# Second block: token halves in turn, and its first feed-forward layer once over both at 512 columns

## The reference

```python
h = x * (1.0 + sc1) + sh1;  hc = xc * (1.0 + csc1) + csh1
y, yc = mixer(h, hc, ...)
x = _layer_norm(ALPHA * x + g1 * y, ln1_g, ln1_b)
h = x * (1.0 + sc2) + sh2
x = _layer_norm(ALPHA * x + g2 * _conv_ffn(h, w_up, conv_w, conv_b, w_down), ln2_g, ln2_b)
if need_ctx:            # first layer only: the same weights over the context's tokens
    xc = _layer_norm(ALPHA * xc + cg1 * yc, ln1_g, ln1_b)
    hc = xc * (1.0 + csc2) + csh2
    xc = _layer_norm(ALPHA * xc + cg2 * _conv_ffn(hc, ...), ln2_g, ln2_b)
```

## Time and profile before

| | |
|---|---|
| median of 3 runs | 2494.47 us (2494.15 to 2495.27) |
| profiled execution: time | 2492.11 us |
| its span | 2490.8 us, 41466 instructions |
| PE busy | 2289.4 us (92%), 18046 instructions |
| DVE / ACT busy | 1322.1 us (53%) / 1129.4 us (45%) |
| weight loads | 355 of 1 MB |
| HBM read | 376.87 MB |

### The profile page before, as it was taken

The page is one execution under the profiler, slowest core; times in us unless marked ns, Lnnn a source line. Parts: engine busy times, 40 slices in busy tenths (PEclk is TensorE's granted clock), DMA queues, the critical chain, the costliest instruction groups (busy, mean ns, idle before and its releaser), DMA issues.

```text
span 2490.8 us, 41466 instructions
## 1 busy us (share of the span) xinstructions
PE 2289.4 (92%) x18046; PEld 2074.7 (83%) x18046; DVE 1322.1 (53%) x1986; ACT 1129.4 (45%) x1754; POOL 54.4 (2%) x100
## 2 busy tenths in 40 slices
PE   6999989998999999899987998689989979997997
PEld 5998779997998899789975766489989956576997
DVE  3446565456555665365554256366666642355665
ACT  3444454436444643364445255254445531344544
POOL 0000000000000100000000000000000000000000
PEclk9999989999999899899998999899999989998999
DMA  8454535545544644255452110145444513203551
GB/s 311 175 190 178 209 138 197 198 158 220 187 170 177 231 172 164 92 204 188 171 203 83 68 51 35 51 152 194 174 166 178 187 67 124 96 18 113 192 191 46
DMA packets 55381, 381.00 MB, mean 153 GB/s; under 512 B 8480, under 2 KB 8864, under 8 KB 9248
## 3 DMA queue, kind: packets, MB, share of 16 engines
q1 hardware_dynamic: 51264, 373.32, 40.2%
q10 hardware_dynamic: 864, 4.63, 0.5%
q0 software_dynamic: 3072, 0.40, 0.1%
HBM read 376.87 MB, written 1.05 MB: 152 GB/s over the span
## 4 chain that ended last, share of the span: by engine, by line
PE 86%; DVE 8%; ACT 4%; DMA 1%; issue 1%; SPq 0%; POOL 0%; DVEq 0%; ACTq 0%
PE ps L551 18%; PE ps L552 17%; PE ps L553 17%; PE ps L682 5%; PE ps L332 3%; PE ps L333 2%; PE ps L334 2%; PE ps L1971 2%; PE ps L1972 2%; PE ps L1973 2%; PE ps L1213 1%; PE ps L748 1%; PE ps L735 1%; DVE wl L306 1%; PE ps L376 1%; PE ps L2241 1%
## 5 line engine op out<-in xcount | busy, mean ns | idle before, releaser
L306 DVE TENSOR_TENSOR wl<-ring,wh 128x1024 fp32r<-128x1024 f32 x538 | 631.2, 1221 | 303.3 <-ACT wh L302 302.8
L551 PE MATMUL ps<-xs,wh 128*128 128x256 f32 x2464 | 704.9, 286 | 57.4 <-DVE wl L306 51.3
L552 PE MATMUL ps<-xs,wl 128*128 128x256 f32 x2464 | 703.3, 285 | 0.0
L553 PE MATMUL ps<-xs,wh 128*128 128x256 f32 x2464 | 703.1, 285 | 0.0
L302 ACT ACTIVATE wh<-ring 128x1024 fp32r<-128x1024 f32 x538 | 534.9, 1049 | 177.4 <-PE ps L553 128.0
L551 PEld LDWEIGHTS ps<-xs,wh 128*128 128x128 f32 x2464 | 479.6, 195 | 61.8 <-DVE wl L306 47.6
L552 PEld LDWEIGHTS ps<-xs,wl 128*128 128x128 f32 x2464 | 479.5, 195 | 0.0
L553 PEld LDWEIGHTS ps<-xs,wh 128*128 128x128 f32 x2464 | 479.3, 195 | 0.0
L551 PE MATMUL ps<-hh,wh 128*128 128x256 f32 x1232 | 348.9, 283 | 2.2 <-DVE hl L649 2.2
L552 PE MATMUL ps<-hh,wl 128*128 128x256 f32 x1232 | 348.6, 283 | 0.0
L553 PE MATMUL ps<-hl,wh 128*128 128x256 f32 x1232 | 348.6, 283 | 0.0
(11 more groups left out here) (381 smaller groups left out, 2927.3 us busy)
## 6 DMA issues: line engine op xcount, KB each, us to landing
ring<-wstream SPq DMA_DIRECT2D x355, 1024.0 KB, 4.9
ada_rows<-ada_stage POOLq DMA_DIRECT2D x96, 4.0 KB, 4.4
CN<-consts ACTq DMA_DIRECT2D x1, 1136.0 KB, 15.5
X<-xin ACTq DMA_DIRECT2D x1, 1024.0 KB, 10.5
X<-cin ACTq DMA_DIRECT2D x1, 1024.0 KB, 9.1
out<-X SPq DMA_DIRECT2D x1, 1024.0 KB, 3.9
PT__59<-pin ACTq DMA_DIRECT2D x1, 512.0 KB, 18.9
ab_w<-wab ACTq DMA_DIRECT2D x1, 512.0 KB, 3.8
```

What stands on the lines that cost most here:

```text
L306: dve.tensor_tensor(wl[:, BUF[i], :, :], tile_of(i), wh[:, BUF[i], :, :].bitcast(F32), ALU.subtract).then_inc(low_part, 1)
L551: pe.matmul(out, wh[:, w, c, :], x_hi, start=start, stop=False, skip_group_check=True)
L552: pe.matmul(out, wl[:, w, c, :], x_hi, start=False, stop=False, skip_group_check=True)
L553: return pe.matmul(out, wh[:, w, c, :], x_lo, start=False, stop=True, skip_group_check=True)
```

## The change

In the second block:

- The output projection of the even mixer runs x's eight tiles and then the context's eight, each 256 columns wide; its third and fourth weight slots get high buffers of their own (`e_wh2`). x's mixer output is split during the last steps of the context's attention. The norm of x (`l0_1x`) is done while TensorE works on the context's tiles, the context's (`l0_1c`) while it works on x's first two gate/up tiles.
- Gain, bias and modulation are folded into one scale and one offset for each feature (`dve_ln_columns`), applied to `Z` directly. ALPHA times the norm's result is made in place in `Z` (`act_residual`).
- The first layer's FFN runs once: gate, up and the first four output blocks of down 512 columns wide over both halves (tiles 0 and 1 of gate/up half by half). PSUM has room for four of the eight output blocks only, so all hidden rows are kept, and the last four blocks are made after the loop, 11 double steps for x, then 11 for the context, 256 columns wide. During the context's steps x's second norm (`l0_2x`) is done; the context's (`l0_2c`) during the odd mixer's first tiles.
- This FFN has four weight buffers, and 40 loads in place of 66.
- `l1_1` takes the form of the first block's norms; in `l1_2` the last eight passes are shared by ScalarE and VectorE.

The core of the diff (new functions, then what calls them):

```diff
-        BUF.append((i - first) % 4 if first <= i < last else i % NB)
+        BUF.append((i - first) % 4 if first <= i < last else (i - both) % 4 if both <= i < both + 7 * NPAIR else i % NB)
         PREV.append(max((j for j in range(i) if BUF[j] == BUF[i]), default=None))
...
+        def dve_modulated_low(name, q):
+            k = x_parts(X_AFTER[name]) // 4 - XSPLITS.index("l0_x")
+            for c in (2 * q, 2 * q + 1):
+                g, b = ln_cols(name, c)
+                dve.wait_ge(z_normed, 4 * LNS.index(name) + q + 1)
+                dve.tensor_scalar(x_whole(name, c), Z[:, ln_half(name), c, :], g, b, ALU.mult,
+                                  ALU.add).then_inc(low_whole, 1)
+            dve.wait_ge(x_high, x_parts(X_AFTER[name]) + q + 1)
+            dve.wait_ge(low_whole, 8 * k + 2 * q + 2)
+            c = slice(2 * q, 2 * q + 2)
+            dve.tensor_tensor(x_target(name, 1, c), x_whole(name, c), x_target(name, 0, c).bitcast(F32),
+                              ALU.subtract).then_inc(x_low, 1)
...
+        def act_residual(name, c0=0, c1=KC):
+            n, j = LN_COLS.index(name[0:4]), ln_half(name)
+            if name in X_AFTER:
+                act.wait_ge(*x_split(X_AFTER[name]))
+                act.wait_ge(x_high, x_parts(X_AFTER[name]) + 4)
+            else:
+                act.wait_ge(h_made, KC)
+            for c in range(c0, c1):
+                z = act.activation(Z[:, j, c, :], Z[:, j, c, :], ACT.Identity, scale=ln_res[:, n, 0, c:c + 1],
+                                   bias=ln_res[:, n, 1, c:c + 1])
+            if c1 == KC:
+                z.then_inc(z_scaled, 1)
...
+            for t in range(16):
+                j = t // 8
                 if t >= 4:
-                    pe.wait_ge(z_done, Z0["l0_1"] + 2 * (t - 3))
-                return t % 4
-            for t in range(8):
-                pe_slot_tile(9 + t // 2, t % 2, bank_out(t), lambda c: e_yh[:, c, :], lambda c: e_yl[:, c, :],
-                             e_y_low if t == 0 else None)
+                    pe.wait_ge(z_done, Z0["l0_1x"] + t - 3)
...
+            def gate_or_up(t, k, j=None):
+                b, i = 4 + 2 * (t % 2) + k, gate_up_tile(t, k)
+                out, x = (ps[:, b, :], slice(0, 2)) if j is None else (ps[:, b, j * T:(j + 1) * T], j)
+                pe.wait_ge(low_part, i + 1)
+                for c in range(KC):
+                    mm = three(out, i, c, xc[:, x, c, 0, :], xc[:, x, c, 1, :], start=(c == 0))
+                return mm
+            def down(t):
+                i = F0 + 5 * (t // 2) + 4
+                pe.wait_ge(low_part, i + 1)
+                pe.wait_ge(hidden_low, G0 + t + 1)
+                for o in range(4):
+                    mm = three(ps[:, o, :], i, 4 * (t % 2) + o, fh[:, t % 2, :, :], fl[:, t % 2, :, :], start=(t == 0))
+                if t % 2:
+                    mm.then_inc(proj_done, 1)
+                elif t == NT - 2:
+                    mm.then_inc(f_down20, 1)
+            def last_down(j, k):
+                i = B0 + NPAIR * j + k
+                pe.wait_ge(low_part, i + 1)
+                pe.wait_ge(f_low, NPAIR * j + k + 1)
+                for o in range(4):
+                    for u in range(2):
+                        mm = three(ps[:, 4 + 2 * j + o // 2, (o % 2) * T:(o % 2 + 1) * T], i, 4 * u + o,
+                                   fh[:, (NPAIR * j + k) % 2, u, :], fl[:, (NPAIR * j + k) % 2, u, :],
+                                   start=(k == 0 and u == 0 and o % 2 == 0))
+                    if k == NPAIR - 1 and o == 1:
+                        mm.then_inc(f_bank, 1)
+                mm.then_inc(proj_done, 1)
+            pe.wait_ge(*x_split("l0_x"))
+            gate_or_up(0, 0, 0)
+            pe_mean("l0_1c")
+            gate_or_up(0, 1, 0)
+            gate_or_up(1, 0, 0)
+            pe_variance("l0_1c")
+            gate_or_up(1, 1, 0)
+            for c in range(KC):
+                if c % 2 == 0:
+                    pe.wait_ge(x_low, x_parts("l0_c") + c // 2 + 1)
+                for k in range(2):
+                    mm = three(ps[:, 4 + k, T:2 * T], gate_up_tile(0, k), c, xc[:, 1, c, 0, :], xc[:, 1, c, 1, :],
+                               start=(c == 0))
+            mm.then_inc(gate_up_done, 1)
+            gate_or_up(1, 0, 1)
+            gate_or_up(1, 1, 1).then_inc(gate_up_done, 1)
+            down(0)
+            for t in range(2, NT):
+                gate_or_up(t, 0)
+                gate_or_up(t, 1).then_inc(gate_up_done, 1)
+                down(t - 1)
+            down(NT - 1)
+            for k in range(NPAIR):
+                last_down(0, k)
+            for k in range(NPAIR):
+                last_down(1, k)
+                if k == 0:
+                    pe_mean("l0_2x")
+                if k == 4:
+                    pe_variance("l0_2x")
...
+            def hidden(t, ahead=()):
+                k, n = t % 2, G0 + t
+                act.wait_ge(gate_up_done, n + 1)
+                act.activation(fcg[:, k, :, :], ps[:, 4 + 2 * k, :].rearrange("p (j n) -> p j n", j=2), ACT.Identity,
+                               scale=pcol("l0_cw", NT + t), bias=pcol("l0_cb", t)).then_inc(conv_mid, 1)
+                for i in ahead:
+                    act_high(i)
+                act.wait_ge(conv_side, 2 * t + 2)
+                act.activation(fsg[:, k, :, :], fcg[:, k, :, :], ACT.Silu).then_inc(silu_done, 1)
+                buf, at = hidden_of(t)
+                act.wait_ge(hidden_done, n + 1)
+                act.activation(fh[:, k, :, :], buf[:, at, :, :], ACT.Copy).then_inc(hidden_high, 1)
+            def last_high(m):
+                j, k = divmod(m, NPAIR)
+                if m == 0:
+                    act.wait_ge(f_down20, 1)
+                else:
+                    name, value = TAKEN[F0 + 5 * NPAIR - 1 if m == 1 else B0 + m - 2]
+                    act.wait_ge(signal[name], value)
+                buf, at = hidden_of(2 * k)
+                act.activation(fh[:, m % 2, :, :], buf[:, at:at + 2, j, :], ACT.Copy).then_inc(f_high, 1)
+            hidden(0, [F0 + 4])
+            act_high(F0 + 5)
+            hidden(1)
+            act_residual("l0_1c")
+            act_high(F0 + 6)
+            act_high(F0 + 7)
+            for t in range(2, NT):
+                hidden(t)
+                i = F0 + 5 * (t // 2)
+                if t % 2 == 0:
+                    act_high(i + 3)
+                    act_high(i + 4)
+                    act_high(i + 5)
+                elif t < NT - 1:
+                    act_high(i + 6)
+                    act_high(i + 7)
+            act.preload_act_table_set("natural_log_exp_and_others")
+            last_high(0)
+            act_high(B0 + 1)
+            act_high(B0 + 2)
+            for m in range(1, 2 * NPAIR):
+                last_high(m)
+                if m + 2 < 2 * NPAIR:
+                    act_high(B0 + m + 2)
+                k = m - NPAIR
+                if k in (1, 2):
+                    act_square("l0_2x", 2 * k - 2)
+                    act_square("l0_2x", 2 * k - 1)
+                if k == 5:
+                    act_factor("l0_2x")
+                if 6 <= k < 10:
+                    act_modulated("l0_2x", 2 * (k - 6))
+                    act_modulated("l0_2x", 2 * (k - 6) + 1)
+            act_residual("l0_2x")
...
+            dve.wait_ge(ln_cols_made, 1)
             for t in range(8):
-                dve_add_branch("l0_out", "l0_1", t, 2, lambda j: MOD[:, 0, 16 + t, j:j + 1])
+                branch(0, t)
+            dve_low(F0)
+            for q in range(4):
+                dve_centre("l0_1x", q)
+            branch(1, 0)
+            for q in range(4):
+                dve_square_pair("l0_1x", q)
+            branch(1, 1)
+            dve_low(F0 + 1)
+            branch(1, 2)
+            dve_scaled("l0_1x", 0)
+            dve_scaled("l0_1x", 1)
+            dve_modulated_low("l0_1x", 0)
+            branch(1, 3)
+            dve_scaled("l0_1x", 2)
+            dve_modulated_low("l0_1x", 1)
+            branch(1, 4)
+            dve_scaled("l0_1x", 3)
+            dve_modulated_low("l0_1x", 2)
+            branch(1, 5)
+            dve_modulated_low("l0_1x", 3)
+            branch(1, 6)
+            branch(1, 7)
+            dve_layer_norm("l0_1c", None, (F0 + 2, F0 + 3))
...
+            z = Z0["l0_2"]
+            last_low(0)
+            dve_low(B0 + 1)
+            dve_low(B0 + 2)
+            dve.wait_ge(z_scaled, ZIN["l0_c"])
+            dve.wait_ge(*tile_done(B0 - 1))
+            for m in range(1, 2 * NPAIR):
+                last_low(m)
+                if m + 2 < 2 * NPAIR:
+                    dve_low(B0 + m + 2)
+                if m <= 4:
+                    for o in (0, 1) if m % 2 else (2, 3):
+                        dve_last_branch((m - 1) // 2, o)
+                if m in (5, 6):
+                    dve_pair("l0_2x", m - 5, z + 2 * (m - 4))
+                k = m - NPAIR
+                if k == 0:
```

(71 more changed lines are left out.)

563 lines of the change are left out of this document (377 added, 186 removed).

## The result

The changed kernel takes 2415.39 us (median of 4 runs, 2413.82 to 2416.07), the kernel before in the same measurement 2494.31 (2494.13 to 2495.27): ratio 0.9683, 95% interval 0.9671 to 0.9695. Forecast were 2418.7 in a range from 2408 to 2440. The gain is 78.9 us, 75.8 were worked out.

A forecast was written before the change was run, and what follows sets the result against it. TensorE was taken to bound the kernel, time being won at its waits or in shorter work. Gains of 68.5 (stretch), 6.8 (norm before the last FFN) and 0.5 (last norm) sum to 75.8, giving 2418.7 us, range 2408 to 2440.

The forecast's parts named there:

- The bound and the pitches: TensorE is 86% of the chain; 512 columns save 12.8 ns a pair, 15.7 us in all; the rest is seams.
- Attention tail: End of context attention: four copies and four subtractions moved into its last steps cost 2.0 us, bounds 0 to 2.8.
- Output projection: Even mixer: 16 tiles take 46.0 us plus 3.75 for statistics; x's norm hidden, ring slot eating 2 of 3 us spare.
- First two tiles: First FFN's gate/up by halves: 23.0 us, 3.75 for the context's statistics, and a 2.8 us wait for its parts.
- Main loop: First-layer FFN: gate/up 217.6 us, down 59.8; weight chain hidden with 1.3 us of slack, no wait, 13.6 us a tile.
- Rival 5: Main loop waits for weights in each tile, each microsecond past 8.2 costing 20; chance 0.04 mild, 0.02 in full.
- Residual: Loop tile one: eight `act_residual` passes ahead of a weight copy in ScalarE's queue make TensorE wait 3.2 us.
- low clock: Two falls of TensorE's clock after waits of 2.5 to 3 us cost 3.0 us, bounds 0 and 9.
- Last down tiles: After the loop: x's and context's last down tiles, waits and extra chain costing 8.0 us, bounds 3 and 20.
- Rivals 2 and 4: Clock falls for good in last context tiles, 2436, chance 0.08; all last down tiles take 4.8 us, 2453, chance 0.05.
- The stretch as a whole: End of even attention to the odd projection's sixth tile: 535.6 us before, 467.1 after, gain 68.5 us.
- Rival 1: Norms aren't hidden at the output projection: two exposed by 9 us each, 2437 us; chance 0.14.

The follow-up runs named there:

- e1: Changed kernel with each 512-column gate/up tile of the loop made as two 256-column halves: 2424.33 us, ratio 0.9720 to the kernel before.
- e5: Changed kernel with the variance of x's first norm made after the output projection's 15th tile instead of the 11th: 2419.76 us, ratio 0.9706 to the kernel before.
- e2b: Changed kernel with three idle ScalarE passes before the next weight copy in loop tiles 2 to 20: 2480.08 us, ratio 0.9944 to the kernel before.
- e3: Changed kernel with the residual's passes done two at a time behind later weight copies, in both FFNs: 2405.20 us, ratio 0.9644 to the kernel before.
- e4: Changed kernel with VectorE's centring and scaling ahead of the weight tile's low part in the context's last down tiles: 2404.59 us, ratio 0.9643 to the kernel before.
- e2a: Changed kernel with one idle ScalarE pass before the next weight copy in loop tiles 2 to 20: 2409.29 us.
- e7: Changed kernel with both the spread residual passes and VectorE's centring and scaling moved ahead in the context's last down tiles: 2399.40 us, ratio 0.9622 to the kernel before.

## Why the prediction was right, point by point

**The bound and the pitches.** Right in the pitches: e1 gives 13.1 ns a pair against 12.8. The 2.5 ns of the Trainium skill ("TensorE: Matmul & The Clock Gate", Back-to-back issue gap), which the page gives for the isolated gap of a matmul and not for a stream with its weight loads, is a fifth of what a pair of these matmuls saves by this trace and by e1. "The rest is seams" was wrong. The norms' statistics got cheaper too, since neighbouring blocks are now added before the matmuls: a mean of l0_2 before, and its context half after the change:

```profile
2018.31 7.03 PE L437 MATMUL ps<-Z,CN 128*128 128x512 f32 x16
```

```profile
1978.43 1.89 PE L509 MATMUL ps<-ln_sum,CN 128*128 128x256 f32 x8
```

Four such rows before and eight after make some 13 us less. The output projection lost 192 pairs, 2.5 us. So of the 78.4 us some 26 are less work for TensorE (16.0 + 13 - 2.5), 46.0 are waits, and most of the rest is low clock (an estimate from the clock over stretches of 1 us: 16 us lost before, 11 after). The forecast gain held in spite of it, because its sum counts the matmuls after the change and takes them from the whole stretch before.

**Attention tail, 2.0.** Mis-sized: 0.49. Most of the passes found idle time, so the truth lay near the lower of the bounds, 0 and 2.8.

**Output projection, 46.0 and 3.75.** Right: 49.60 us from 1537.48 to 1587.08, no wait. The x half was ready 48.6 us into the stretch, 1.0 before it was wanted, which is the forecast's 3 less the 2 that the ring slot eats. What was expected of e5 took the 3 as if nothing ate of it.

**First two tiles.** The wait before the context half is 1.6 in three pieces, not 2.8: the parts come 2.05, 2.04 and 1.44 us apart after the first, not 2.2. The first FFN matmul was forecast for 1588.6 and came at 1587.08.

**Main loop.** Right in its place and in its size: no wait, 13.6 us a tile, slack 1.1 to 1.4 where 1.3 had been worked out. What the forecast had wrong about the loop is the price beyond the edge: "each microsecond costs 20" is 37 by e2b (67.5 us for 1.81), since most waits have a fall of the clock behind them. Rival 5 was as unlikely as I said, but nearly twice as dear.

**Residual, 3.2; end of the loop, 2.5; low clock, 3.0.** 2.61, 2.58 and about 1.6 (one fall, 0.58 for 4.07 us; after the second wait of the same length the clock stayed at 1.00). e3 shows that the residual's eight passes are the cause of the first.

**Last down tiles, 8.0.** Measured 5.8 in five waits (0.51, 1.48, 1.07 and 1.35 in four of them), the later tiles 4.45 apart against 4.8 forecast. The mechanism was right, and e4 takes it away by order alone. Rivals 2 and 4 have fallen: the clock was 1.00 all through, and only five tiles waited. The Trainium skill's case of short idle spells (same page, A second HAM failure mode: psum-queue depth-cycling) doesn't strike at this spacing; in e2b's loop, with a wait of 1.81 us a tile, the clock did swing.

**The stretch as a whole.** 73.0 gained, 68.5 forecast. The waits and passes that were put too high (1.5 attention, 1.2 context half, 0.6 residual, 2.2 last tiles, 1.4 clock) are 6.9 us less than the sum. Of this 2.4 were given back: some 1.7 between the first FFN matmul and the end of the loop, 0.9 in the last down tiles and 0.2 at the end of the attention, less some 0.5 by which the two projections stayed under their terms. Most of it is one thing, that a listed wait is shorter than what it costs: before the one of 1.07 us two starts are 1.35 apart (1958.81 and 1960.16) where 0.12 is the pitch, and the next start comes after 0.19. That is 0.23 us for each, at five waits in the last tiles and six before them.

**After it.** Not forecast: 1.3 us lost in the odd mixer, where nothing was changed. The tile behind its 3.03 us wait, before the change:

```profile
2142.00 8.80 PE L682 MATMUL ps<-sg,ring 128*128 128x512 f32 x16 [3.03 <-DVE m_k L2398]
```

After it, it takes 10.07, behind the same wait. The norm before the last FFN gave 9.5 where 9.8 were worked out, and 3.6 of it came back where the residual was put at 3.0 (a wait of 1.94, and low clock): 5.9 for 6.8. The last norm gave 0.8 for 0.5.

**Rival 1**, norms exposed, is the one that had a real mechanism (e5); it stayed out by 1.0 us.

**Small slips.** From the rows 29.3 less 19.3 is 10.0 for the norm before the last FFN, where the forecast has 9.8. The costs between bounds, all taken one way, reach from about 2397 to 2444, not from 2406 to 2442.

In spans the gain is 2.6 more than forecast: 4.5 in the terms of the stretch and 0.3 in the last norm, less 1.3 of clock that no step had named and 0.9 at the norm before the last FFN. The other 0.7 of the 3.3 us in the medians is the distance between profiled execution and median. That the miss is so small is in part luck: errors of both signs met, and the clock in parts that were not changed moved other variants of this kernel by more than the whole miss.

## What to carry to other kernels

Where a queue serves both the next tile and a norm beside it, put the passes that release the other engine ahead of the ones that are wanted a tile later; here that order alone was worth 5.9 us. Size a hidden chain by its slack, and past the slack count each wait and the clock behind it: a loop that was 1.81 us a tile too slow lost 3.6. Compare variants between marks around the edit, not by their totals, since an unchanged part of this kernel moved by up to 5 us.

## What the runs showed of the hardware

Waits with the same length and the same releaser were followed by different granted clocks. After 3.02 or 3.03 us before the m_k tile: 0.71 in the changed kernel (10.04 us for 16 matmul instructions), 1.00 in e2a (7.10), and 8.80 us in e4, e7 and the kernel before (8.76 in e2b). After 2.58 to 2.61 us in the changed kernel: 0.58 at tile two, 1.00 at the end of the loop; in e3 and e7, which have no wait at tile two, the fall stands at the end of the loop, and e1 has one at both (after 2.3 and 2.56). In e2b 16 of 19 waits of 1.81 us had a fall behind them, at a cost of 1.6 us each, while five waits of 0.5 to 1.5 us in the last context tiles had none. What decides between them is left open; how the waits lie in time against what ran before them is a guess that no run here separated.
